# First keys projected chunk by chunk among the last modulation groups, and a second gate projected at the head of the merge

## What is computed

```python
mod = silu(c) @ w_mod[layer] + b_mod[layer]              # 6 x 1024; mod_c the same for the context
h = rms_norm(x, norm_mix[layer]) * (1 + scale1) + shift1  # h_ctx the same with mod_c
q, k, v, hy, g = split(h @ w_in[layer])                  # 8 query heads, 2 key heads, 2 value heads
attn = latent_attention(q, k, v, kc, vc)                 # layer 0 also attends within the context
hyo = hyena_mix(hy, ...)                                 # a short and a long convolution
g_attn, g_hyena = split(sigmoid(g))
merged = g_attn * (attn @ w_o_attn) + g_hyena * (hyo @ w_o_hyena)
x = x + gate1 * (merged @ w_out)                         # then a SwiGLU feed-forward part
```

## Time and profile before

| what | us |
|---|---|
| median of three timed runs | 2030.71 (2029.64 to 2033.61) |
| time of the profiled execution | 2027.09 |
| its span | 2025.3 |
| PE busy | 1854.4 (92%) |
| DVE busy | 1136.5 (56%) |
| ACT busy | 910.6 (45%) |
| granted TensorE clock, mean | 0.97 |

### The profile page before, as it was taken

How to read it: one execution, slowest core, us unless ns; L and a number is a source line. 1 busy time by engine, 2 the same in 40 slices (tenths; PEclk the granted TensorE clock), 3 DMA queues, 4 the chain that set the end, 5 groups by cost and what they waited for, 6 DMA issues and landing times.

```text
span 2025.3 us, 33662 instructions
## 1 busy us (share of the span) xinstructions
PE 1854.4 (92%) x14064; PEld 1521.8 (75%) x14064; DVE 1136.5 (56%) x1877; ACT 910.6 (45%) x1582; POOL 16.9 (1%) x31
## 2 busy tenths in 40 slices
PE   7999989999999999999999999999999876677676
PEld 4877668888778888889799999997798744444342
DVE  3555767776786778658856667779765200000001
ACT  4333345665766667555555555743844200000001
POOL 0000000000000000000000000000000000000000
PEclk8999999999999999999999999999999989888899
DMA  8222014553555666325156556556166999999997
GB/s 320 94 73 83 11 69 150 185 180 101 178 177 182 192 191 195 104 76 175 32 156 210 169 186 197 179 192 214 63 244 247 387 419 421 419 419 421 421 420 302
DMA packets 95121, 427.95 MB, mean 211 GB/s; under 512 B 10097, under 2 KB 16754, under 8 KB 71282
## 3 DMA queue, kind: packets, MB, share of 16 engines
q1 hardware_dynamic: 82866, 382.45, 51.6%
q10 hardware_dynamic: 12096, 43.26, 6.7%
HBM read 424.62 MB, written 1.05 MB: 210 GB/s over the span
## 4 chain that ended last, share of the span: by engine, by line
PE 70%; DMA 15%; DVE 5%; SPq 4%; ACT 4%; issue 2%; ACTq 0%; POOL 0%; DVEq 0%
PE bank L545 41%; PE bank L1761 8%; SPq L2984 3%; DMA con<-in_w 3%; DMA area<-in_w 3%; DMA ring<-in_w 2%; PE bank L1273 2%; PE bank L2621 2%; PE bank L1244 2%; PE bank L560 2%; DMA ahead<-in_w 1%; DMA X<-in_w 1%; DMA his<-in_w 1%; DMA HH<-in_w 1%; PE bank L2258 1%
## 5 line engine op out<-in xcount | busy, mean ns | idle before, releaser
L524 DVE TENSOR_TENSOR ring_r<-ring,his_r 128x1024 fp32r<-128x1024 f32 x314 | 383.4, 1223 | 217.9 <-ACT his_r L516 216.7
L545 PE MATMUL bank<-HH_r,his_r 128*128 128x256 f32 (+1 forms) x1472 | 485.1, 330 | 3.5 <-DVE ring_r L524 3.5
L545 PE MATMUL bank<-HH_r,ring_r 128*128 128x256 f32 (+1 forms) x1472 | 477.5, 324 | 0.0
L516 ACT ACTIVATE his_r<-ring 128x1024 fp32r<-128x1024 f32 x314 | 330.8, 1056 | 287.2 <-PE bank L545 255.6
L545 PE MATMUL bank<-H_r,his_r 128*128 128x256 f32 (+1 forms) x1408 | 458.4, 326 | 0.0
L545 PEld LDWEIGHTS bank<-HH_r,his_r 128*128 128x128 f32 x1472 | 277.9, 189 | 34.9 <-issue 10.5
L545 PEld LDWEIGHTS bank<-HH_r,ring_r 128*128 128x128 f32 x1472 | 277.8, 189 | 24.1
L545 PEld LDWEIGHTS bank<-H_r,his_r 128*128 128x128 f32 x1408 | 264.8, 188 | 24.4 <-issue 1.0
L2637 DVE TENSOR_TENSOR tmp<-tmp,bank 128x128 f32<-128x128 f32 x64 | 18.4, 288 | 366.7 <-ACT tmp L2630 254.9
L545 PE MATMUL bank<-area_r,his_r 128*128 128x256 f32 (+1 forms) x480 | 148.6, 322 | 4.8 <-DVE ring_r L524 4.8
L1761 PE MATMUL bank<-VT_r,his_r 128*128 128x512 f32 (+1 forms) x352 | 117.2, 333 | 0.3 <-DVE YF_r L1488 0.3
(11 more groups left out here) (449 smaller groups left out, 3432.1 us busy)
## 6 DMA issues: line engine op xcount, KB each, us to landing
area<-in_w SPq DMA_DIRECT2D x63, 1024.0 KB, 27.3
ring<-in_w_in SPq DMA_DIRECT2D x102, 512.0 KB, 3.5
ring<-in_w_gate_up SPq DMA_DIRECT2D x88, 512.0 KB, 3.6
ring<-in_w SPq DMA_DIRECT2D x24, 1024.0 KB, 27.0
ring<-in_w_down SPq DMA_DIRECT2D x44, 512.0 KB, 3.5
ahead<-in_w SPq DMA_DIRECT2D x18, 1024.0 KB, 27.7
X<-in_w SPq DMA_DIRECT2D x16, 1024.0 KB, 27.1
HH<-in_w SPq DMA_DIRECT2D x16, 1024.0 KB, 26.8
```

Of the source, the lines that this page charges most:

```text
L516: ac.eng.activation(hi_slot(n), stream.slot(u), ACT.Copy).then_inc(*ac_hi.up(n))
L524: ve.eng.tensor_tensor(lo_slot(u), stream.slot(u), hi_slot(n).bitcast(F32), ALU.subtract).then_inc(*ve_lo.up(n))
L545: ins = pe.eng.matmul(out, a, b, start=k == 0 and m == 0, stop=end)
```

## The change

It has two parts. In the first stage, the columns of `w_mod` are put in another order, so that group g holds shift and scale of chunks 2g and 2g+1. `ve_mod_first(g)` makes them ready behind the turn of group g. The key weights are laid out so that one unit holds chunks 0 to 3 of both key heads, and the next one chunks 4 to 7. The second key unit is loaded behind the last `w_mod` unit instead of ahead of four of them. PE does half of group 3, then key chunks 0 and 1, the other half, key chunk 2, the turn of group 3, and the remaining chunks; the 24 idle matmuls are gone. ACT and DVE have orders of their own for this stage, written out. The last `w_mod` units go to other free tiles, since `HH` is now written earlier. `pe_keys_projected` serves both layers.

In the merge of both layers, the second attention gate (ga of j = 1, unit 26 of `w_in`) is projected first, ahead of oa of j = 0, and the stream has its unit ahead of the first `w_o_attn` unit. Within the attention before it, ACT splits this unit one step earlier than it did the first `w_o_attn` unit (DVE in the same step as before), and the `w_o_attn` unit is split at the start of `ac_merge` and `ve_merge`. In layer 0 no attention head is cut within the attention any more; all 8 are cut in the merge. In layer 1 four are still cut within the attention.

```diff
+MOD_COLUMNS = [j for g in range(4) for j in (2 * g, 2 * g + 1, 8 + 2 * g, 9 + 2 * g)]
         for j in range(8):
-            units += [("w_in", l, 24 + 2 * j), ("w_in", l, 25 + 2 * j), ("w_o_attn", l, j)]
+            units += [("w_in", l, 24 + 2 * j)] if j != 1 else []
+            units += [("w_in", l, 25 + 2 * j)]
+            units += [("w_in", l, 26)] if j == 0 else []
+            units.append(("w_o_attn", l, j))
...
-                       [hh_flat[:, i * UF:(i + 1) * UF] for i in range(4)] + [KX_flat[:, :]], [sem(f"s_m{i}") for i in range(16)], UB)
+                       [ahead[0][:, i * UF:(i + 1) * UF] for i in range(2)] + [KX_flat[:, :], VX_flat[:, :], vt_flat[:, 0:UF]],
+                       [sem(f"s_m{i}") for i in range(16)], UB)
...
-        def pe_mod_group(pe, g):
-                banks.hold((ve_mod, ("added", 0, 0)), "mods")
+                banks.hold((ve_mod, ("first", 3, 1)), "mods")
+            if half != 1:
+                banks.hold((ac_mod, ("rows", g)), "mod", g)
+                pe.wait_ge(*banks.emptied("mod", g))
+                pe.wait_ge(*ve_mod.at("silu", 1))
+            for k in range(8) if half is None else range(4 * half, 4 * half + 4):
...
-            ins.then_inc(*pe_mod.up("group", g))
-            if g > 0:
-                pe_mod_turn(pe, g - 1)
-            if g == 3:
-                pe_mod_turn(pe, g)
-                banks.give("mods")
+            if half != 0:
+                ins.then_inc(*pe_mod.up("group", g))
+                banks.give("mod", g)
         def pe_mod_turn(pe, g):
+            if g:
+                pe.wait_ge(*ve_mod.at("first", g - 1, 1))
-                j = 4 * g + n
+                j = MOD_COLUMNS[4 * g + n]
...
+        def ve_mod_first(ve, g):
+            ve.wait_ge(*landed["vec"])
+            ve.wait_ge(*pe_mod.at("turn", g))
+            for part in range(2):
+                j = 8 * part + 2 * g
...
+                ve.eng.tensor_tensor(MODS[0][:, j:j + 2, :], src, vv(("b_mod", 0), j, 2).unsqueeze(2).to_broadcast([P, 2, 2]),
+                                     ALU.add).then_inc(*ve_mod.up("first", g, part))
...
+        def ac_first_norm(ac):
+            ac_split(ac, where["w_in", 0, 0])
+            ac_norm_chunk(ac, "mix0", 0, 512, 0)
+            ac_mod_group(ac, 2)
+            for k in range(1, 5):
+                ac_norm_chunk(ac, "mix0", 0, 512, k)
+            ac_split(ac, where["w_in", 0, 1])
+            ac_mod_group(ac, 3)
+            for k in range(5, 8):
+                ac_norm_chunk(ac, "mix0", 0, 512, k)
...
+        def ve_first_norm(ve):
+            ve_mod_first(ve, 0)
+            r = ve_rstd(ve, "mix0", 512)
+            ve_scaled(ve, "mix0", 0, 512, r)
+            ve_scaled(ve, "mix0", 1, 512, r)
+            ve_split(ve, where["w_in", 0, 0])
+            ve_scaled(ve, "mix0", 2, 512, r)
+            ve_mod_first(ve, 1)
+            ve_low(ve, "mix0", 0, 512)
+            ve_scaled(ve, "mix0", 3, 512, r)
+            ve_low(ve, "mix0", 1, 512)
+            ve_mod_first(ve, 2)
+            ve_scaled(ve, "mix0", 4, 512, r)
+            ve_low(ve, "mix0", 2, 512)
+            ve_scaled(ve, "mix0", 5, 512, r)
+            ve_low(ve, "mix0", 3, 512)
+            ve_split(ve, where["w_in", 0, 1])
+            ve_low(ve, "mix0", 4, 512)
+            ve_mod_first(ve, 3)
+            ve_scaled(ve, "mix0", 6, 512, r)
+            ve_low(ve, "mix0", 5, 512)
+            ve_scaled(ve, "mix0", 7, 512, r)
+            ve_low(ve, "mix0", 6, 512)
+            ve_low(ve, "mix0", 7, 512)
...
+        def pe_chunk_ready(pe, l, k):
+            if l == 0 and k == 2:
+                pe_mod_group(pe, 3, 1)
+            if l == 0 and k == 3:
+                pe_mod_turn(pe, 3)
+            pe.wait_ge(*ve_norm.at("low", f"mix{l}", k))
+
+        def pe_keys_projected(pe, l):
+            out = [head_bank(pe, l, i) for i in range(2)]
+            for k in range(8):
+                pe_chunk_ready(pe, l, k)
+                for h in range(2):
+                    w, i = stream.block("w_in", l, 8 * pos[8] + 2 * k + h)
...
+                    stream.spent[i] = (pe_products, ("keys_half", l) if k < 4 else ("head", l, h))
+                    ins.then_inc(*pe_products.up("keys_half", l))
...
-            pe_pair(pe, [(("head", l, i), head_bank(pe, l, i), 8 * pos[8 + i]) for i in range(2)], "w_in", l,
-                    lambda k: (HH[:, k, 0:512], HL[:, k, 0:512]), lambda k: pe.wait_ge(*ve_norm.at("low", f"mix{l}", k)))
+            pe_keys_projected(pe, l)
...
-                return None
-            return h - (4 if l == 0 else 5)
+            return h - 5 if l else None
+
+        def second_gate_now(l, n, h):
+            return n == 1 - l and h == (4 if l else 3)
...
             def side(ac, h):
                 convolve(ac, h)
                 k = merge_cut_now(l, n, h)
-                if k == 0:
-                    ac_split(ac, unit("w_o_attn", l, 0))
+                if second_gate_now(l, n, h):
+                    ac_split(ac, unit("w_in", l, 8 * pos[25]))
                 if k in range(4):
-                    ac.wait_ge(*ve_soft.at("out", "att1" if l else "ctx0", k, 0))
-                    ac.wait_ge(*ve_conv.at("out", l, 0 if l else 1, 3))
+                    ac.wait_ge(*ve_soft.at("out", "att1", k, 0))
...
-                if k == 0:
-                    ve_split(ve, unit("w_o_attn", l, 0))
+                if second_gate_now(l, n, h - 1):
+                    ve_split(ve, unit("w_in", l, 8 * pos[25]))
...
 
             for j in range(8):
-                if j:
-                    ga = banks.take((ac_out, ("ga", l, j)), "ga", l, j)
-                    gh = banks.take((ac_out, ("gh", l, j)), "gh", l, j)
-                else:
+                if j == 0:
                     banks.give("ga", l, 0)
                     banks.give("gh", l, 0)
+                gates = ((("ga", 1, 25),), (("gh", 1, 33),))[j] if j < 2 else (("ga", j, 24 + j), ("gh", j, 32 + j))
+                gates = [(key, n, b, banks.take((ac_out, (key, l, n)), key, l, n)) for key, n, b in gates]
...
@@ -1543,11 +1623,12 @@
 
         def ac_merge(ac, l):
             t, site = tokens(l), "att1" if l else "ctx0"
+            ac_split(ac, unit("w_o_attn", l, 0))
...
-            for k in range(4, 8):
+            for k in range(4 if l else 0, 8):
                 ac_cut_tile(ac, hi_att(k, l), ATT[:, k, 0:t], ("att", l, k))
...
-            for k in range(4, 8):
+            ve_split(ve, unit("w_o_attn", l, 0))
+            for k in range(4 if l else 0, 8):
                 ve_cut_tile(ve, hi_att(k, l), ATTL[:, k, 0:t], ATT[:, k, 0:t], ("att", l, k))
...
         def tensor_program(pe):
             pe_mod_group(pe, 0)
             pe_mod_group(pe, 1)
+            pe_mod_turn(pe, 0)
             pe_open(pe, "mix0")
             pe_added("mix0")
             pe.wait_ge(*gp_start.at("ones"))
@@ -2993,8 +3076,9 @@
             pe_sum_last(pe, "mix0", 512)
             pe_spread(pe, "mix0", 512)
             pe_mod_group(pe, 2)
-            pe_mod_group(pe, 3)
-            pe_idle(pe, "mix0", 12)
+            pe_mod_turn(pe, 1)
+            pe_mod_group(pe, 3, 0)
+            pe_mod_turn(pe, 2)
...
                     sp.eng.dma_start(X[:, :, :], T["x"]).then_inc(*landed["x"])
                 if i == 12:
                     weights(0)
-                    weights(1)
                 sp.eng.dma_start(first.slot(i), T[name][l, u]).then_inc(first.arrived(i)[0], 16)
+            weights(1)
...
-        "w_in": tiles(np.concatenate([halves(I["w_in"][:, :, 0:1280]), I["w_in"][:, :, 1280:]], axis=2), paired(W_IN_ORDER, 8, (10,))),
+        "w_in": tiles(np.concatenate([halves(I["w_in"][:, :, 0:1280]), I["w_in"][:, :, 1280:]], axis=2), paired(W_IN_ORDER, 8, (8, 10))),
```

More of the change, by code:

```diff
@@ L680, in two_blocks_kernel, with pe_mod_group @@
         rmod = PP
-        def pe_mod_group(pe, g):
+        def pe_mod_group(pe, g, half=None):
             if g == 0:
-                banks.hold((ve_mod, ("added", 0, 0)), "mods")
-            out = banks.take((ac_mod, ("rows", g)), "mod", g)
-            pe.wait_ge(*banks.emptied("mod", g))
-            pe.wait_ge(*ve_mod.at("silu", 1))
-            for k in range(8):
+                banks.hold((ve_mod, ("first", 3, 1)), "mods")
[4 more added lines that the diff above has]
+            for k in range(8) if half is None else range(4 * half, 4 * half + 4):
                 w, u = first.block("w_mod", 0, 32 * g + 4 * k, 4)
@@ L710, in pe_mod_turn @@
             ins.then_inc(*pe_mod.up("turn", g))
+            if g == 3:
+                banks.give("mods")
         def ac_mod_group(ac, g):
@@ L734, in ve_mod_scale, with modulated @@
                                             ALU.mult).then_inc(*ve_mod.up("scale", l, part, s))
-        def modulated(l, part):
-            return ve_mod.at("scale", l, part, 1)
+        def modulated(l, part, k):
+            return ve_mod.at("scale", l, part, 1) if l or part else ve_mod.at("ready", k // 2, 1)
```

(40 more changed lines are left out.)

49 lines of the change are left out of this document (19 added, 30 removed).

## The result

| kernel | median, us | executions | profiled execution, span |
|---|---|---|---|
| before | 2030.2 | 4 (2028.3 to 2033.6) | 2027.09, 2025.3 |
| changed | 2013.3 | 4 (2011.6 to 2016.8) | 2016.79, 2015.0 |

The ratio is 0.9917 [0.9898, 0.9936]: faster by 13 to 21 us, 17 by the medians. The forecast was 2018.7 with a range from 2014.5, so the direction was right and the time lies just outside. Two later comparisons of the same kernel gave 15.0 and 15.4 us (0.9922 [0.9905, 0.9939], 0.9924 [0.9911, 0.9938]).

A forecast was written before the change was run, and what follows sets the result against it. It took PE (70% of the chain of waits, transfers 15%) to bound the kernel until the experts. Terms 4.5 + 2.1 + 3.1 + 2.3 = 12.0 us off the 2030.71 median gave 2018.7, range 2014.5 to 2026.0.

The forecast's parts named there:

- Part 1: First stage: keys interleaved with the last modulation groups start and end earlier; -4.5 us, bounds -1.3 and -4.6.
- 30.51 + 4.0 = 34.5: First stage: keys finish as if started in one piece at 34.5 instead of 39.12, a gain of 4.6 us.
- The bound of −4.6: Far bound of the keys' gain in the first stage, if nothing makes PE wait.
- Light work lowered it: PE's clock in the first stage: turns and small sums lowered it, wide products raised it; new order's light work costed at nothing.
- 0.234 each, 11.2 for 48: Keys in the first stage: 45 matmuls in 10.55 us, so 11.2 for 48; keys end near 45.7.
- the rival of the hand-overs: Keys: hand-overs between engines bind, keys give 1.3 us; sum 8.8, time 2021.9; chance 0.12.
- Part 2: Layer 0's context attention: ACT splits one step earlier and four cuts leave; -2.1 us, bounds -1.0 and -2.8.
- Part 3: Layer 0's merge: cut wait gone, `w_o_hyena` wait 1.5 instead of 2.4; -3.1 us, bounds -1.2 and -4.0.
- Part 4: Layer 1's merge: wait for `w_o_hyena` unit 0.7 in place of 2.41; -2.3 us, bounds -1.0 and -2.9.
- The slower rival: Clock low through keys and values: +14.4 us, time 2045; for one short stretch 1 to 2 us lost; chance 0.05.
- The rival of merges that give half: Both layers' merges: DVE's late hyena split keeps PE waiting; they give 1.2 + 1.0, time 2021.9; chance 0.12.
- the one in which the end swallows the gain: Experts' stage: transfers run at their own pace, independent of PE; time 2030, within the noise; chance 0.08.

The follow-up runs named there:

- after_third: The changed kernel unchanged, timed again beside the repeat of cuts_back: 2015.81 us, ratio 0.9924 to the kernel before.
- after_again: The changed kernel unchanged, timed once more to tell scatter from effect: 2015.02 us, ratio 0.9922 to the kernel before.
- cuts_back: The changed kernel with layer 0's cuts of attention heads 0 to 3 put back in steps 4 to 7 of the context attention: 2012.37 us, ratio 0.9914.
- unit_ahead: The changed kernel with the second key unit loaded ahead of the last `w_mod` units again: 2017.41 us, one execution.
- before_again: The kernel before, unchanged, timed against itself: 2029.64 us, ratio 1.0003.
- before_warm: The kernel before with 16 idle matmuls between the first two modulation groups and 2 ahead of the spread: 2031.85 us against 2031.22, ratio 1.0007.
- merge_only: The kernel before with only the second part (stream order, second gate ahead, merge), first stage as before: 2022.82 us, ratio 0.9961.
- warm: The changed kernel with two bursts of matmuls that nothing reads (16 and 2 calls) in the first stage: 2014.63 us, ratio 0.9928.
- keys_only: The kernel before with only the first part (modulation columns, keys, first-stage orders), attention and merge as before: 2019.42 us, ratio 0.9957.
- best: cuts_back with the two bursts of warm: 2011.74 us, ratio 0.9918 to the kernel before.
- cuts_back_again: The same kernel as cuts_back, timed again beside the changed kernel: 2016.94 us, ratio 0.993 to the kernel before.
- the small row loads: Kernel before and changed kernel, each with modulation row loads from the 27th on cut to 32 of 1024 columns: 5962.6 and 5947.2 us.

## Why the prediction was outside its range

**Part 1, keys, −4.5: the step that failed.** It set the keys' start at "30.51 + 4.0 = 34.5", and cost the clock "at nothing". The 30.51 was read from a trace with the clock at 0.55 in 26 to 30, where nothing depended on it, since the keys waited for a transfer. Taken as PE's floor in the new order it holds the slow products within it. At 1.00, spread and group 2 take 2.5 us less (5.55 to 3.01), and the values start 6.7 us earlier. after_third shows the term as it was meant: PE reaches the half group at 30.57 with a clock of 0.55 in 26 to 30, the clock is 1.00 behind it, and the values start 4.6 us earlier (47.39). A second fall, in after_again, leaves 3.0. Over the ten executions with the new start in the table it was 3.0 to 6.9, 5.3 on average (52.0 less 46.7). The bound of −4.6 was none; what bounds the term at a full clock is the landing of the units of group 3 (28.3). I saw the clock as a risk only, and gave the side on which it would gain nothing. "Light work lowered it" isn't a rule either: the changed kernel and cuts_back did the same light work in 20 to 23 us and kept 1.00 to 30. "0.234 each, 11.2 for 48" took 45 records for 45 matmuls; the 10.55 us are those of all 48, so the keys' end should have read 45.1, and the difference of 4.6 isn't touched. Moving the key unit gave nothing at the clock of unit_ahead; at a full clock I estimate 1.1 us for it. No wait of PE stands between chunks, so the rival of the hand-overs fell.

**Part 2, attention, −2.1:** −2.02 in every execution with the new merge order. Right, with its mechanism.

**Part 3, merge of layer 0, −3.1:** −2.91, with a wait of 1.46 where 1.5 was forecast. Right as far as the merge goes. "In this stretch PE is busy 16.00 of 16 us ... so DVE catches up" looked 16 us on and not at the stage behind, where the row loads took 3 us back in the profiled executions.

**Part 4, merge of layer 1, −2.3:** −2.32. The wait left is 0.24, not 0.7; the sum was right.

**The base and the scatter.** That the time came out 1.2 us beyond the edge, 2014.5, is partly luck. The two repeats, 15.0 and 15.4 us faster than the kernel before beside them, taken from 2030.2, give 2015.2 and 2014.8, just inside. The four terms as measured, with the keys at 5.3 to 6.7, come to 12.5 to 13.9, against 15.0 to 16.9 by the medians; less the 3 us behind merge 0 the profiled executions differ by 10.3. The profiled execution of the kernel before lay 2 to 5 us under the median of its others (before_again, before_warm), and that of the changed one 4.0 to 4.7 above (three times; merge_only 5.3, warm 4.3). Those with a short stretch behind merge 0 lay under theirs too: keys_only 2.8, cuts_back 7.1, best 1.8; cuts_back_again, with 137.83 there, lay on its median. With the small row loads it lies about 2 above in both, and the two ways of comparing agree (16.0 and 15.4). This speaks for a loss behind merge 0 that profiled executions of the new order have and the others mostly don't; no run shows it, since only profiled executions have a trace. The rest, 1 to 4 us by the terms, stays open. One stretch that I hadn't looked at varies by as much: from the end of layer 1's gate and up products to the 168 matmuls ahead of the experts the profiled executions take 307.2 to 311.6 us, the kernel before 310.5 and 309.0, the changed one 309.3, 310.4 and 311.0. It follows no edit; what sets it isn't shown.

**The other rivals.** The end passed everything on: from the 168 products that start at 1503.27 in the kernel before and at 1494.20 in the changed one to the end it is 522.0 and 520.8 us, and 520.5 to 522.2 in all executions whose chain shows them. The expert stage's share answers to the earlier trace rows:

```profile
1620.00:1990.00 370.00, 262.37 (x3814) 159.24 (x3807) 26.41 (x105) 30.91 (x89) 0.00 (x0) 0.87 1.01 420
```

The slower rival, a clock low through keys and values, didn't come. Its short form, "1 to 2 us", did: after_again starts its values 1.7 us behind after_third. Counted from the full clock, which I hadn't priced, it is 3.75. The rival of merges that give half fell (parts 3 and 4), and so did the one in which the end swallows the gain.

## What to carry to other kernels

A start time read from a trace in which that engine didn't set the pace holds whatever slack it had, a lower clock among it; before it is used as a floor in a new order, its wide products are costed at the higher level too, as the near end of the range, and the next transfer behind it is looked up as the new bound. Where a wait goes at the head of a stage, look for the next place that is tied to a transfer's landing, not only at the next few us. And gains of one or two us between variants need a repeat side by side: 2.7 us of cuts_back were gone in the second comparison.

## What the runs showed that I had not expected

The same program meets different clocks. In 26 to 30 us the changed kernel had 1.00, 0.57 and 0.55 in its three profiled executions, the kernel before 0.55 and 0.80, with the same instructions in the same order.

The 576 matmuls of gate and up in layer 1 take either 65.3 to 65.5 us or 67.8 to 68.1, whatever the kernel (before 65.28, changed 67.84 and 68.08, then 65.28; before_warm 68.07). Within one such stretch the value is the same for all, but it can change between stages: in the changed kernel the merge just ahead ran at the shorter one, 720 matmuls in 82.53 us, 0.115 each. One line's groups in 1130 to 1170 us (engine, operation, tiles, count, duration in ns as min/median/max), the kernel before and the changed one:

```profile
L545 PE MATMUL bank<-HH_r,his_r x119: 276/276/276, 1129.8 to 1169.9; 128*128 128x256 f32 x119
```
```profile
L553 PE MATMUL bank<-HH_r,his_r x114: 281/281/281, 1129.9 to 1169.9; 128*128 128x256 f32 x114
```

The 576 matmuls in 65.28 and 67.84 us are 113 and 118 ns each, with PE busy throughout these 40 us and a granted clock of 1.00 in both. It is 2.6 us of scatter that belongs to no edit, and it is why spans of single executions don't rank kernels that lie this close.
